# Gate/up units two at a time, joined key projections, and a reordered start and end of the SSD stage in a two-layer hybrid decoder kernel

## What is computed

```python
for i in range(DEPTH):
    x = x + 0.5 * swiglu(rmsnorm(x), ffn_w_gate_up[i, 0], ffn_w_down[i, 0])
    h = rmsnorm(x)
    x = x + (short_conv_mixer(h) if i % 2 == 0 else ssd_mixer(h))
    x = x + memory_cross_attn(rmsnorm(x), rmsnorm(mem), w_q, w_kv, w_o)
    x = x + 0.5 * swiglu(rmsnorm(x), ffn_w_gate_up[i, 1], ffn_w_down[i, 1])
return rmsnorm(x)
# ssd_mixer: z, xbc, dt = split(h @ w_in); xbc = silu(conv4(xbc) + bias)
#   decay[l, s] = exp(a_cum[l] - a_cum[s]) for s <= l; y = (C B^T * decay) @ (x dt) + state part
#   y = groupwise rmsnorm(y * silu(z)) * gate_norm; return y @ w_out
# memory_cross_attn: 4 heads of 256; softmax(q k^T / 16) @ v, then w_o
```

## Time and profile before

| what | value |
|---|---|
| median of 3 runs | 1286.51 us (1286.28 to 1286.92) |
| profiled execution, its own time | 1286.15 us |
| its span | 1284.3 us |
| PE busy | 1273.5 us, 99% of the span |
| PEld busy | 1154.2 us, 90% |
| DVE busy | 998.9 us, 78% |
| ACT busy | 760.5 us, 59% |
| POOL busy | 237.0 us, 18% |

### The profile page before, as it was taken

One profiled execution on the slowest core, in us unless ns is written; L12 is line 12 of the kernel. 1 busy time (PEld: TensorE's weight loads), 2 busy tenths in 40 slices (PEclk: granted clock), 3 DMA queues, 4 the chain that ended last, 5 costly groups with the idle time before them and its releaser, 6 DMA issues.

```text
span 1284.3 us, 23538 instructions
## 1 busy us (share of the span) xinstructions
PE 1273.5 (99%) x8074; PEld 1154.2 (90%) x8074; DVE 998.9 (78%) x1554; ACT 760.5 (59%) x1374; POOL 237.0 (18%) x311
## 2 busy tenths in 40 slices
PE   9999999999999999999999999999999999999997
PEld 8888888899999888888888888999999989888887
DVE  6888778897668888668888678998977767888754
ACT  6655554555556656545556447878865656565642
POOL 2433110122002111111111112024421201111111
PEclk9999999999999999999999999999999999999999
DMA  8556645655445556645556647644445544555660
GB/s 282 185 184 211 204 160 173 196 186 177 151 132 191 185 194 207 206 162 171 188 185 224 197 151 263 222 153 132 132 140 195 187 157 140 181 183 192 225 199 37
DMA packets 62806, 232.52 MB, mean 181 GB/s; under 512 B 6992, under 2 KB 7568, under 8 KB 62608
## 3 DMA queue, kind: packets, MB, share of 16 engines
q1 hardware_dynamic: 62080, 230.73, 54.8%
q10 hardware_dynamic: 656, 0.86, 0.2%
HBM read 230.49 MB, written 1.08 MB: 180 GB/s over the span
## 4 chain that ended last, share of the span: by engine, by line
PE 96%; DVE 2%; ACT 1%; issue 0%; DMA 0%; POOL 0%; ACTq 0%; DVEq 0%
PE bank L1419 94%; DVE w_lo L822 1%; DMA raw<-w_gu 0%; PE bank L1767 0%; PE bank L1579 0%; PE bank L1739 0%; DVE t L822 0%; ACT w_hi L400 0%; PE bank L1519 0%; DVE root_n L825 0%; DVE root_n L822 0%; PE bank L1794 0%; DVE rms_n L825 0%; DVE acc L822 0%; ACT gate L453 0%
## 5 line engine op out<-in xcount | busy, mean ns | idle before, releaser
L822 DVE TENSOR_TENSOR w_lo<-raw,w_hi 128x1024 fp32r<-128x1024 f32 (+2 forms) x403 | 524.0, 1303 | 42.7 <-ACT w_hi L400 41.4
L400 ACT ACTIVATE w_hi<-raw 128x1024 fp32r<-128x1024 f32 (+2 forms) x403 | 441.8, 1098 | 35.8 <-PE bank L1419 27.8
L1419 PE MATMUL bank<-h,w_hi 128*128 128x512 f32 (+1 forms) x1808 | 447.1, 385 | 0.5 <-DVE w_lo L822 0.3
L1419 PE MATMUL bank<-a,w_hi 128*128 128x256 f32 (+1 forms) x1878 | 386.7, 324 | 0.3 <-DVE w_lo L822 0.2
L1419 PEld LDWEIGHTS bank<-h,w_hi 128*128 128x128 f32 x1808 | 321.3, 189 | 54.5 <-DVE h L825 0.8
L1419 PEld LDWEIGHTS bank<-a,w_hi 128*128 128x128 f32 x1878 | 310.8, 190 | 24.8 <-issue 0.5
L1419 PE MATMUL bank<-a,w_lo 128*128 128x256 f32 x1280 | 260.6, 283 | 0.0
L1419 PEld LDWEIGHTS bank<-h,w_lo 128*128 128x128 f32 x1736 | 242.1, 190 | 16.7
L1419 PE MATMUL bank<-h,w_lo 128*128 128x256 f32 x1736 | 254.7, 282 | 0.0
L400 ACT ACTIVATE corr<-bank 128x256 f32<-128x256 f32 x239 | 91.1, 382 | 267.2 <-PE bank L1419 267.2
L1419 PEld LDWEIGHTS bank<-a,w_lo 128*128 128x128 f32 x1280 | 204.5, 191 | 4.8
(11 more groups left out here) (193 smaller groups left out, 1063.6 us busy)
## 6 DMA issues: line engine op xcount, KB each, us to landing
raw<-w_gu SPq DMA_DIRECT2D x174, 512.0 KB, 4.2
raw<-w_down SPq DMA_DIRECT2D x64, 704.0 KB, 4.2
raw<-w_xbc SPq DMA_DIRECT2D x32, 512.0 KB, 4.1
raw<-w_conv_in SPq DMA_DIRECT2D x24, 512.0 KB, 3.8
raw<-w_q SPq DMA_DIRECT2D x16, 512.0 KB, 4.4
raw<-w_k SPq DMA_DIRECT2D x16, 512.0 KB, 3.5
raw<-w_v SPq DMA_DIRECT2D x16, 512.0 KB, 3.5
raw<-w_o SPq DMA_DIRECT2D x16, 512.0 KB, 3.8
```

Of the source, the lines that this page charges most:

```text
L400: return nc.scalar.activation(out, in_, ACT.Copy, scale=scale)
L822: return nc.vector.tensor_tensor(out, a, b, op)
L1419: return nc.tensor.matmul(out, lhs, rhs, start=start, stop=stop, skip_group_check=check)
```

## The change

Five edits, with what each one moves:

1. In the loops of gate/up on PE, `two_units` replaces two calls of `pair_unit`: the products with `w_hi` of both units first, then those with `w_lo`. It waits for `hi_ready` ahead of the high products and for `lo_ready` ahead of the low ones. There are 9 turns of the loop in the first SwiGLU and 10 in each of the other three, two pairs a turn, 78 pairs.
2. The 16 key units become `pair_unit`. ACT gets a `corr_copy` for each, DVE adds the correction and then multiplies by `rms_mem` in an instruction of its own (`key_scaled`). The scores and the softmax stand one step later.
3. The turned y of the last group goes to bank 7. Its `yt` waits for the last `y_added` in place of `yt_ready`. On DVE the weight split of that step stands behind the root of the last group.
4. `decays_by` gives 3 pairs in two steps in place of 4, and the last two pairs of 16 move into the xbc steps: `diffs` at t = 0 and 1, `decays` at t = 1 and 2.
5. The norm ahead of the SSD takes its last square straight into PE (four more products of 2 columns), as the first and the last norm do, so POOL makes one addition less.

```diff
-            if name[:4] == "down" or name[:2] == "gu" or name in ("conv_in", "q0"):
+            if name[:4] == "down" or name[:2] == "gu" or name in ("conv_in", "q0") or name in ("k0", "k1"):
...
-            return KT - 2 if b in (0, NORM_FINAL) else KT - 1
+            return KT - 2 if b in (0, NORM_MIX1, NORM_FINAL) else KT - 1
...
+        LATE_PAIRS = PAIRS - 2
...
-            return min(PAIRS, max(0, 2 * (s - 5)))
+            return min(LATE_PAIRS, max(0, (3 * (s - 5) + 1) // 2))
...
+        def turn_bank(g):
+
+            return bank[5 if g < GROUPS - 1 else 7]
...
# ScalarE
-                        if s == 11 + 2 * h:
+                        if s == 12 + 2 * h:
...
-                        b, use = bank_use(f"k{layer}", s - KT)
-                        act.wait_ge(evac[b], use + 1)
+                        corr_copy(s % 4, s, n0 + s)
+                        act.wait_ge(key_scaled, KT * layer + s - KT + 1)
                         copy(k_hi[:, s - KT, :], gate[s % 2][:, :]).then_inc(kv_hi, 1)
...
                     if 0 < t <= 4 * GROUPS:
                         silu_xbc(*divmod(t - 1, 4))
+                    if t and LATE_PAIRS + t <= PAIRS:
+                        decays(LATE_PAIRS + t - 1)
...
# VectorE
-                        dve.wait_ge(unit_done, n0 + s + 1)
+                        b, use = bank_use(f"k{layer}", k)
                         if k >= 2:
                             dve.wait_ge(kv_hi, KV_PARTS * layer + k - 1)
-                        tt(gate[s % 2][:, :], bank[s % 4][:, 0:N_MEM], rms_mem[:, :]).then_inc(evac[s % 4], 1)
+                        dve.wait_ge(corr_ready, pair_first[f"k{layer}"] + k + 1)
+                        tt(gate[s % 2][:, :], bank[b][:, 0:N_MEM], corr[s % 2][:, :], ALU.add).then_inc(evac[b], 1)
+                        dve.wait_ge(evac[b], use + 1)
+                        tt(gate[s % 2][:, :], gate[s % 2][:, :], rms_mem[:, :]).then_inc(key_scaled, 1)
...
-                    if t < SSD_UNITS and q != 3:
-                        split(nx + t + AHEAD)
                     if ("root", t) in due and due["root", t] >= LAST_ROOT:
                         g = due["root", t]
                         dve.wait_ge(ysq_ready, 2 * g + 2)
                         inverse_root(rms_y[:, g % 2, :], var_y[:, g % 2, :], sum_y[:, g % 2, :], root_y[:, g % 2, :], 1.0 / GW).then_inc(rmsy_ready, 1)
                         normed_y(g)
+                    if t < SSD_UNITS and q != 3:
+                        split(nx + t + AHEAD)
...
+                    if LATE_PAIRS + t < PAIRS:
+                        diffs(LATE_PAIRS + t)
...
# TensorE
+            def two_units(n, name, t, i):
+
+                outs = []
+                for u in range(2):
+                    outs.append(free(name, t + u, i=i))
+                    pe.wait_ge(hi_ready, n + u + 1 + SLOTS * i)
+                    for k in range(KT):
+                        mm(outs[u][:, :], w_hi[(n + u) % SLOTS][:, k * P:k * P + P], h[:, :, k, :], k == 0, False)
+                for u in range(2):
+                    pe.wait_ge(lo_ready, n + u + 1 + SLOTS * i)
+                    for k in range(KT):
+                        ins = mm(outs[u][:, SEQ:], w_lo[(n + u) % SLOTS][:, k * P:k * P + P], h[:, 0, k, :], False, k == KT - 1)
+                    ins.then_inc(unit_done, 1)
...
-                    for s in range(4):
-                        pair_unit(n0 + s, free(name, s, i=i), KT, 0, h, True, True, i)
+                    for s in (0, 2):
+                        two_units(n0 + s, name, s, i)
...
-                        unit(n0 + s, free(f"k{layer}", t), KT, 0, mn, True, True,
+                        pair_unit(n0 + s, free(f"k{layer}", t), KT, 0, mn, True, True,
...
-                        if s == 10 + 2 * h:
+                        if s == 11 + 2 * h:
...
-                        at_least(pe, yt_ready, 2 * g)
+                        if g < GROUPS - 1:
+                            at_least(pe, yt_ready, 2 * g)
+                        else:
+                            pe.wait_ge(y_added, GROUPS)
```

More of the change, by code:

```diff
@@ L211, in trunk @@
         kv_hi, k_ready = sem("kv_hi"), sem("k_ready")
+        key_scaled = sem("key_scaled")
         scaled_ready = sem("scaled_ready")
@@ L683, in ssd @@
                 evict_z(3)
-                for j in range(lcount, PAIRS):
+                for j in range(lcount, LATE_PAIRS):
                     decays(j)
@@ L695, in ssd @@
                             j = 2 * g + u
-                            copy(a_hi[:, j, :], bank[5][:, u * SEQ:u * SEQ + SEQ], col(C_GATE, j)).then_inc(yhi_ready, 1)
+                            copy(a_hi[:, j, :], turn_bank(g)[:, u * SEQ:u * SEQ + SEQ], col(C_GATE, j)).then_inc(yhi_ready, 1)
                     if G < GROUPS:
@@ L1209, in ssd @@
                             j = 2 * g + u
-                            stt(a_lo[:, j, :], bank[5][:, u * SEQ:u * SEQ + SEQ], col(C_GATE, j),
+                            stt(a_lo[:, j, :], turn_bank(g)[:, u * SEQ:u * SEQ + SEQ], col(C_GATE, j),
                                 a_hi[:, j, :].bitcast(F32), op1=ALU.subtract).then_inc(yt_ready, 1)
@@ L1738, in ssd @@
                             for c in range(2):
-                                ins = nc.tensor.transpose(bank[5][:, u * SEQ + c * P:u * SEQ + c * P + P],
+                                ins = nc.tensor.transpose(turn_bank(g)[:, u * SEQ + c * P:u * SEQ + c * P + P],
                                                           y[g % 2][:, c, u * P:u * P + P], cst[:, C_EYE:C_EYE + P])
```

## The result

The changed kernel takes 1288.95 us (median; 1286.79 to 1290.72) against 1286.57 us for the kernel before, run beside it: a ratio of 1.0018, 95% interval 1.001 to 1.0027. That is inside the 0.2% that a measurement can just tell, but on the slow side, where I had forecast 1285.5 us.

The account below looks back on a forecast made before the run. PE, busy 1273.5 of 1284.3 us, was taken to bound the kernel. Gains of 4.3 less losses of 3.4 left 0.9 us less, forecast as 1285.5 us from the median; the forecast case ran from 1284.0 to 1286.9.

Parts of the forecast that it names:

- the losses, put down at 3.4 us: Whole kernel: 0.4 us for layer 0's keys plus 3.0 us of PE waiting for x of group 0.
- the table-load sum for x of group 0: First xbc steps: 6.2 us more on ACT, less cover, lead and idle time, plus 0.3, leaves PE waiting 3.0 us.
- its term for ACT's lead: First xbc steps: ACT begins `acc` 1.5 us sooner, bounds 1.2 and 4, with two pairs of differences no longer ahead.
- Gate/up in pairs: Gate/up loops on PE: fewer changes of product width gain 0.018 us a pair, 78 pairs, 1.4 us; bounds 0 and 3.
- Joined keys: Key units of both layers: 2.88 to 2.793 us each, 16 units, a gain of 1.4 us; bounds 1.2 to 1.5.
- In layer 0 ... I give 0.4 us: Layer 0 keys: ACT and DVE fall behind, delaying the last scores by 0.4 us; bounds 0 and 2 for both layers.
- End of the SSD: Last y turning: bank 7 and the moved split remove PE's wait, a gain of 1.1 us; bounds 0.8 and 1.2.
- the attribution to bank 5 against the name in the row: Last y turning: PE's wait ends with group 6's low part, still read from bank 5, though the rows name y.
- Norm: Norm ahead of the SSD: POOL's dropped addition frees DVE's root a little, a gain of 0.1 us; bounds 0 and 0.4.
- Start of xbc, 0.3 us: First xbc unit: two pairs of differences less ahead on DVE remove PE's wait for low weights, 0.3 us gained.
- the rival of the dearer switch: Table switches on ACT: running empty adds 1.3 us for each of four, 5.2 us more, giving 1290.7; chance 0.04.
- that of the hidden loads: Start of xbc: ACT is 4 us ahead, so PE waits only 0.5 us for x, giving 1283.0; chance 0.25.

Follow-up runs that it names:

- Edit 4 alone: The kernel before with only the late decay differences added (three pairs in two steps, last two pairs in the xbc steps): 1291.82 us, ratio 1.0042.
- fill_seven: The changed kernel with seven unused float32 products of ones put into bank 7 ahead of PE's first wait for x: 1287.29 us, ratio 1.0005.
- early_pairs: The changed kernel with the late decay pairs wholly undone (two pairs a step, all 16 in the z steps): 1283.49 us, ratio 0.9977.
- the repeated run: The changed kernel, unchanged, measured and profiled again: 1289.16 us, ratio 1.0017; its profiled execution took 1288.42 us.
- one_switch: The changed kernel with both late exponentials at step 2, behind the silu for C, so two table loads fewer: 1286.02 us, ratio 0.9996.
- the two executions after it: Two more profiled executions of the changed kernel, unchanged: 1287.96 and 1287.78 us.

## Why the prediction was wrong

The forecast was 1285.5 us (its own sum gives 1285.6), and the direction was wrong: the gains were there, and the losses, put down at 3.4 us, were 5.2 in waits and some 1.7 more at the median, most of it in the clock. The step that failed is the table-load sum for x of group 0, in its term for ACT's lead; the clock, which the sum had at nothing, comes on top.

- **Gate/up in pairs: right.** 0.018 a pair predicted, 0.020 measured; the high parts came in time. Besides, the wait of 0.28 us at 35.31 went.
- **Joined keys: the product gain was right** (8 units of layer 1: 0.77 us, predicted 0.70). **"In layer 0 ... I give 0.4 us" was mis-sized**: 1.15 us in two waits, less the 0.2 that stood before the scores in the kernel before, so 0.95. I had allowed the shortfall on the last scores alone, and the softmax was late from the third head on.
- **End of the SSD: right**, 1.1 us, and the attribution to bank 5 against the name in the row too. **Norm**: 0.2 alone, but 0.04 on top of edit 4 (a z stage of 49.19 and 49.15 us); predicted 0.1.
- **Start of xbc, 0.3 us: right in size, by luck in the row.** Edit 4 alone shortens the z stage from 49.52 to 49.19 us, by the short stop ahead of the first xbc product. The wait of 0.3 us in the earlier trace rows that I took for it stands at 35.31, in the first SwiGLU, and went with edit 1.
- **"ACT starts its first `acc` sooner ... I take 1.5 us, bounds 1.2 and 4" failed.** `acc` starts at 816.13 against 817.52, but 0.77 of these 1.4 us is what the whole kernel had gained by then: ACT's own lead is 0.6 us, under my lower bound. Two pairs less did bring 1.54 us; what I had put at nothing is the other half of the same edit, the slower spread of the remaining pairs, which took 0.94 back. The loads had their row's price, 1.29 us start to start, and no drain beside it: the rival of the dearer switch falls, and so does that of the hidden loads. Counted from the start of the stage the last silu ends 4.06 + 0.77 = 4.83 us later; less 1.0 of cover, plus 0.36 by which PE comes sooner, this is 4.2 us, the sum of the two waits. My 3.0 was 1.2 short, of which 0.9 is the lead.
- **A place that I had not looked at.** I followed the loads to x alone. The silu for C is one switch earlier and had 1.8 us of cover in the kernel before; the waits came as 1.0 and 3.3. The 3.3 agrees with my 3.0 only because PE had already stood for 1.0.
- **No term for the clock.** Even with all waits right the sum would have been 1286.8. TensorE's granted clock fell behind the wait of 3.3 us in three of four profiled executions, which cost 1.5 to 1.6 us. The Trainium skill ("TensorE: Matmul & The Clock Gate", section "Why this matters for your kernels") warns of throughput drops behind idle gaps between bursts of matmuls; the trace agrees, and I should have made it a rival as soon as my own sum had a gap of 3 us in it.

From the profiled execution's own time: forecast 1285.25, measured 1286.79. The 1.5 us are 1.2 of x and C, 0.55 of keys and 0.5 of the later start at 23.04, less 0.6 gained more on the pairs, the wait at 35.31 and the keys' products (together 1.65). The median adds 1.7 us more above that execution than in the kernel before, and `fill_seven` takes 1.7 to 1.9 back.

**Still open**: 10 of the 21 timed executions of the changed kernel are above 1289 us, up to 1290.72. One stretch of 3.4 us does not reach that from 1286.8. Their granted clock is given as 0.996 in 7 of the 10, where the two shortest have 0.998; 0.002 of 1285 us would be some 5 us at the lower level, an estimate that suggests a longer or a second stretch. The figure is coarse, though: one execution of 1289.38 us has 0.998, and so has the profiled one of edit 4 alone, with its stretch. No execution above 1289 us of the changed kernel was profiled.

## What to carry to other kernels

Moving a function that needs another table between two that don't costs the loads of each switch, so follow the delay to every consumer in order, not only to the last. An edit that both drops work and spreads the rest more slowly has two prices; here they were 1.5 us gained and 0.9 lost on the engine that mattered. When a stage's start is compared, take out what the whole kernel had gained by then; only the rest is lead. And an engine that sets the pace pays twice for a wait of some us: once for the wait, and, where it is TensorE, perhaps once more for the clock behind it; seven useless products bought back most of the second price. Leaving the exponentials where they had been (`early_pairs`) bought back both.

## What the runs showed of the hardware

- After a wait of TensorE of 3.1 us (in `one_switch` 2.2) the granted clock was at its lower level for about 3.4 us, in four of five profiled executions with the longer wait; the same kernel had it in three executions and not in a fourth. A 256-column product then steps 0.213 in place of 0.120 us. Behind the waits of 0.8 to 0.9 us it was not.
- In the repeated run the steps lengthened only around 833.0, when PE had been at work again since 831.90; in the two executions after it they were long from 0.2 and 0.6 us behind the start of that turning.
- A plain float32 product of 256 columns came as two records of 0.218 us each, 0.436 us together, against 0.120 us for one product of the split operands.
